# Three stages of a two-block transformer begin the next stage's dense product before they end

## What is computed

```
hn = rmsnorm(h)
proj = hn @ w_in                                   # dq dk dv dz da db sq sk sv gate_dn gate_sb
o_dn = rmsnorm(gated_delta_rule(q, k, v, g, beta)) * silu(dz)          # 8 heads of 256, in two groups
o_sb = stick_breaking_attention(rmsnorm(sq), rmsnorm(sk), sv)          # 8 heads of 128
merged = sigmoid(gate_dn) * (o_dn @ w_branch_dn) + sigmoid(gate_sb) * (o_sb @ w_branch_sb)
h = h + merged @ w_out
h = h + (silu(gate) * up) @ w_ffn_out              # gate, up = rmsnorm(h) @ w_ffn_in
```

## Time and profile before

| | |
|---|---|
| median of 3 runs | 2320.32 us (2319.63 to 2327.05) |
| span of the profiled execution | 2316.6 us |
| PE busy | 2205.7 us, 95% |
| DVE busy | 1116.4 us, 48% |
| ACT busy | 806.4 us, 35% |
| transfers | 218.65 MB, mean 94 GB/s |

### The profile page before, as it was taken

The page is one execution under the profiler, slowest core; times in us unless marked ns, Lnnn a source line. Parts: engine busy times, 40 slices in busy tenths (PEclk is TensorE's granted clock), DMA queues, the critical chain, the costliest instruction groups (busy, mean ns, idle before and its releaser), DMA issues. The chain is left out here.

```text
span 2316.6 us, 32721 instructions
## 1 busy us (share of the span) xinstructions
PE 2205.7 (95%) x13572; PEld 1700.6 (73%) x13572; DVE 1116.4 (48%) x1800; ACT 806.4 (35%) x1310; POOL 67.8 (3%) x88
## 2 busy tenths in 40 slices
PE   8999799999999999989998999998999999999999
PEld 7776457777778898976765788766566578888887
DVE  3464675666653367654334534436332244444422
ACT  3332554333332443332224222225346533223221
POOL 0000001000000000000000000000012102000000
PEclk8999899999999999999999999999999999999999
DMA  4224001222232244331224321214721232322322
GB/s 161 65 72 154 1 1 64 82 91 82 87 105 92 78 145 130 124 110 59 66 69 146 130 92 62 70 55 150 247 69 55 91 115 91 95 96 91 98 94 91
DMA packets 78595, 218.65 MB, mean 94 GB/s; under 512 B 8688, under 2 KB 13168, under 8 KB 78448
## 3 DMA queue, kind: packets, MB, share of 16 engines
q1 hardware_dynamic: 78448, 216.57, 28.2%
HBM read 185.74 MB, written 29.75 MB: 93 GB/s over the span
## 5 line engine op out<-in xcount | busy, mean ns | idle before, releaser
L296 PE MATMUL ps<-nx_hi,whi 128*128 128x264 f32 (+1 forms) x1504 | 539.1, 358 | 17.0 <-DVE nx_lo L385 9.6
L281 DVE TENSOR_TENSOR wlo<-raw,whi 128x1024 fp32r<-128x1024 f32 x282 | 346.3, 1228 | 400.4 <-ACT whi L274 400.0
L298 PE MATMUL ps<-nx_hi,wlo 128*128 128x264 f32 (+1 forms) x1504 | 512.9, 341 | 0.0
L297 PE MATMUL ps<-nx_lo,whi 128*128 128x264 f32 (+1 forms) x1504 | 512.8, 341 | 0.0
L274 ACT ACTIVATE whi<-raw 128x1024 fp32r<-128x1024 f32 x282 | 297.8, 1056 | 520.9 <-PE ps L298 416.5
L296 PEld LDWEIGHTS ps<-nx_hi,whi 128*128 128x128 f32 x1504 | 287.0, 191 | 84.6 <-issue 45.3
L298 PEld LDWEIGHTS ps<-nx_hi,wlo 128*128 128x128 f32 x1504 | 287.1, 191 | 32.6
L297 PEld LDWEIGHTS ps<-nx_lo,whi 128*128 128x128 f32 x1504 | 287.7, 191 | 30.4 <-issue 1.9
L296 PE MATMUL ps<-x_hi,whi 128*128 128x512 f32 x528 | 209.8, 397 | 14.9 <-DVE wlo L281 14.9
L298 PE MATMUL ps<-x_hi,wlo 128*128 128x512 f32 x528 | 209.8, 397 | 0.0
L297 PE MATMUL ps<-x_lo,whi 128*128 128x512 f32 x528 | 208.4, 395 | 0.0
(11 more groups left out here) (460 smaller groups left out, 2869.9 us busy)
## 6 DMA issues: line engine op xcount, KB each, us to landing
raw<-stream_dram SPq DMA_DIRECT2D x285, 512.0 KB, 3.5
qk_spill<-ring SPq DMA_DIRECT2D x16, 264.0 KB, 2.2
qk_cols<-qk_spill SPq DMA_DIRECT2D x16, 264.0 KB, 4.0
v_spill<-ring SPq DMA_DIRECT2D x16, 264.0 KB, 2.1
v_cols<-v_spill SPq DMA_DIRECT2D x16, 264.0 KB, 4.3
dz_spill<-ring SPq DMA_DIRECT2D x16, 256.0 KB, 2.1
dz<-dz_spill SPq DMA_DIRECT2D x16, 256.0 KB, 5.1
sbk_spill<-ring SPq DMA_DIRECT2D x8, 264.0 KB, 2.1
```

The costliest lines, as they stand in the source:

```text
L281: dve.tensor_tensor(K.wlo[:, n % HL], K.raw[:, n % RAW], K.whi[:, n % HL].bitcast(F32), ALU.subtract).then_inc(K.s_lo, 1)
L296: pe.matmul(out, whi, xhi, start=start, stop=False, skip_group_check=skip)
L297: pe.matmul(out, whi, xlo, start=False, stop=False, skip_group_check=skip)
L298: return pe.matmul(out, wlo, xhi, start=False, stop=stop, skip_group_check=skip)
```

## The change

A new lane, `Begun`, stands in three stages. It issues matmuls of the next stage's first two outputs with six of their eight contraction tiles (at the end of DeltaOutput 0, 2, 1, 3, 4 and 6, the first that it makes; else 0 to 5), 18 for each output, without a stop, and the next stage's product leaves these out and ends the sums: 6 matmuls for each of its first two outputs. The three places are the end of DeltaOutput (for SecondBranch), of StickBreaking (for LastBranch) and of LastBranch (for `out_ffn`). `Begun` waits for the chunk, for the bank, and for each contraction tile. At the end of DeltaOutput and StickBreaking the banks are 6 and 7, which the stage's own dense product must have left; in LastBranch they are 0 and 1, and nothing holds them. In StickBreaking the first of the two outputs has a time just before the last values, the other one behind all.

So that the operand of LastBranch is there in time, StickBreaking now makes both parts itself: ACT copies a head's bank into `o_hi`, DVE takes the difference of bank and `o_hi` into `o_lo`, two heads at a time. SplitOutputs, with its 8 copies and 8 differences, is gone, and so are the waits of LastBranch's first output. No load is moved from one stage to another.

```diff
...
 
-def out_ffn(K, x_hi, x_lo, nk, conv, gain_ffn, gain_next, out):
+def out_ffn(K, x_hi, x_lo, nk, conv, gain_ffn, gain_next, out, begun=None):
 
...
                     bank_free(d)
-                    for k in range(nk):
+                    skipped = begun.over(s) if begun is not None else ()
+                    for k in range(len(skipped), nk):
                         w = slice((w0 + k) * P, (w0 + k + 1) * P)
                         mm = three(pe, K.ps[:, d % 4, :], K.whi[:, s % HL, w], K.wlo[:, s % HL, w], x_hi[:, k], x_lo[:, k],
-                                   k == 0, k == nk - 1)
+                                   k == 0, k == nk - 1, len(skipped) > 0)
                     if d % per == per - 1:
...
 
-    def __init__(self, K, n, operand, banks, z, t0, t1, led=0):
+    def __init__(self, K, n, operand, banks, z, t0, t1, led=0, begun=None):
         super().__init__(t0, t1)
+        self.begun = begun
         self.K, self.first, self.n, self.operand, self.banks, self.led = K, K.at, n, operand, banks, led
...
                 q = self.base[c] + h
-                for k in range(KT):
+                skipped = self.begun.over(s) if self.begun is not None else ()
+                left = [k for k in range(KT) if k not in skipped]
+                for k in left:
                     yield self.at((c + (h + k / KT) / len(rng)) / self.n)
-                    if h == 0 and k == 0:
+                    if h == 0 and k == left[0]:
                         pe.wait_ge(K.s_lo, s + 1)
-                    if k == 0 and q >= len(self.banks):
+                    if k == left[0] and q >= len(self.banks):
                         pe.wait_ge(self.free, q - len(self.banks) + 1)
                     mm = three(pe, K.ps[:, self.bank(c, h), 0:e - a], K.whi[:, s % HL, k * P:(k + 1) * P],
-                               K.wlo[:, s % HL, k * P:(k + 1) * P], xh[:, k, a:e], xl[:, k, a:e], k == 0, k == KT - 1, True)
+                               K.wlo[:, s % HL, k * P:(k + 1) * P], xh[:, k, a:e], xl[:, k, a:e], k == 0, k == left[-1], True)
                 if h == len(rng) - 1:
...
 
+class Begun(Lane):
+
+
+
+    def __init__(self, K, x_hi, x_lo, a, e, tiles, ready, outs):
+        super().__init__(1e6, 1e6)
+        self.K, self.x_hi, self.x_lo, self.a, self.e = K, x_hi, x_lo, a, e
+        self.tiles, self.ready, self.outs, self.first = tiles, ready, outs, K.at
+
+    def over(self, s):
+        return self.tiles if s < self.first + len(self.outs) else ()
+
+    def pe(self, pe):
+        K = self.K
+        for q, (bank, t, free) in enumerate(self.outs):
+            s = self.first + q
+            yield t
+            pe.wait_ge(K.s_lo, s + 1)
+            if free is not None:
+                pe.wait_ge(*free)
+            for i, k in enumerate(self.tiles):
+                pe.wait_ge(self.ready, i + 1)
+                three(pe, K.ps[:, bank, 0:self.e - self.a], K.whi[:, s % HL, k * P:(k + 1) * P], K.wlo[:, s % HL, k * P:(k + 1) * P],
+                      self.x_hi[:, k, self.a:self.e], self.x_lo[:, k, self.a:self.e], i == 0, False, True)
+
+
 class Stored(Products):
...
 
+    def tile_order(self):
+        return [2 * (2 * j + p) + f for j, f, p in self.ORDER]
+
     def sp(self, sp):
...
 
-    def __init__(self, K, o_hi, o_lo, first_part, gate, dst, c, banks, z, t0, t1):
+    def __init__(self, K, o_hi, o_lo, first_part, gate, dst, c, banks, z, t0, t1, begun):
         self.src, self.dst = (first_part, gate), dst
...
         self.loaded, self.taken, self.stored = [z["branch_in_0"], z["branch_in_1"]], z["branch_taken"], [z[s] for s in STORED_SEMS]
-        super().__init__(K, 8, lambda c: (o_hi, o_lo, [(0, SEQ)]), banks, z, t0, t1)
+        super().__init__(K, 8, lambda c: (o_hi, o_lo, [(0, SEQ)]), banks, z, t0, t1, begun=begun)
 
...
 
-STICK_SEMS = ("z", "ln", "softplus", "later", "log_w", "sw", "pv", "so")
+STICK_SEMS = ("z", "ln", "softplus", "later", "log_w", "sw", "pv", "so_hi", "so")
 
...
 
-    def __init__(self, K, qT, kT, v, z, c, t0, t1):
+    def __init__(self, K, qT, kT, v, o_hi, o_lo, z, c, t0, t1):
         super().__init__(t0, t1)
-        self.K, self.qT, self.kT, self.v, self.s = K, qT, kT, v, z
+        self.K, self.qT, self.kT, self.v, self.o_hi, self.o_lo, self.s = K, qT, kT, v, o_hi, o_lo, z
         self.units = [x for h in range(0, SB_H, 2) for x in [(h + j, a) for j in range(2) for a in (3, 2, 1, 0)] + [(h, TT)]]
...
         K, s = self.K, self.s
+
+        def copy_lo(h):
+            dve.wait_ge(s["so_hi"], h + 1)
+            dve.tensor_tensor(self.o_lo[:, h], K.ps[:, 3 + h % 3, :], self.o_hi[:, h].bitcast(F32), ALU.subtract).then_inc(s["so"], 1)
         for u in range(self.NU):
...
                                      ALU.max, ALU.add).then_inc(s["softplus"], 1)
+            if u >= self.PER and u % self.PER == 2:
+                for j in range(2):
+                    copy_lo(2 * (u // self.PER - 1) + j)
+        yield self.t1
+        for j in range(2):
+            copy_lo(SB_H - 2 + j)
 
...
             act.wait_ge(s["pv"], self.PER * (h // 2 + 1))
-            act.activation(self.qT[:, h, 0:SEQ], K.ps[:, 3 + h % 3, :], ACT.Copy).then_inc(s["so"], 1)
+            act.activation(self.o_hi[:, h], K.ps[:, 3 + h % 3, :], ACT.Copy).then_inc(s["so_hi"], 1)
         act.preload_act_table_set("natural_log_exp_and_others")
...
 
-class SplitOutputs(Lane):
-
-
-    def __init__(self, K, src, hi, lo, z, t0, t1):
-        super().__init__(t0, t1)
-        self.K, self.src, self.hi, self.lo, self.made, self.done = K, src, hi, lo, z["so_hi"], z["so_lo"]
-
-    def act(self, act):
-        for i in range(8):
-            act.activation(self.hi[:, i], self.src[:, i], ACT.Copy).then_inc(self.made, 1)
-        yield from ()
-
-    def dve(self, dve):
-        for i in range(8):
-            dve.wait_ge(self.made, i + 1)
-            dve.tensor_tensor(self.lo[:, i], self.src[:, i], self.hi[:, i].bitcast(F32), ALU.subtract).then_inc(self.done, 1)
-        yield from ()
-
-
 class LastBranch(Products):
...
 
-    def __init__(self, K, o_hi, o_lo, merged, gate, c, banks, z, t0, t1):
+    def __init__(self, K, o_hi, o_lo, merged, gate, c, banks, z, t0, t1, begun):
         self.src = (merged, gate)
...
         self.s = z
-        super().__init__(K, 8, lambda c: (o_hi, o_lo, [(0, SEQ)]), banks, z, t0, t1)
-
-    def pe(self, pe):
-        for k, t in enumerate(super().pe(pe)):
-            if k < KT:
-                pe.wait_ge(self.s["so_lo"], k + 1)
-            yield t
+        super().__init__(K, 8, lambda c: (o_hi, o_lo, [(0, SEQ)]), banks, z, t0, t1, begun=begun)
 
...
             z = named_sems(K, PRODUCT_SEMS, STORED, OUT_SEMS)
-            together(K, DeltaOutput(K, S, o_hi, o_lo, D2["dz"], 8, z, c2, 0, 8),
-                     Stored(K, [(8, XQ, D2["gdn"], 0, rs, (ACT.Tanh, 0.5))], ring, (6, 7), z, 0, 8, 1))
+            output = DeltaOutput(K, S, o_hi, o_lo, D2["dz"], 8, z, c2, 0, 8)
+            dense = Stored(K, [(8, XQ, D2["gdn"], 0, rs, (ACT.Tanh, 0.5))], ring, (6, 7), z, 0, 8, 1)
+            begun = Begun(K, o_hi, o_lo, 0, SEQ, output.tile_order()[0:6], z["o_free"], [(6, 1e6, (dense.free, 7)), (7, 1e6, (dense.free, 8))])
+            together(K, output, dense, begun)
         qT = S.v.rearrange("p m j n -> p (m j n)").rearrange("p (h t) -> p h t", h=8)
...
                 z = named_sems(K, PRODUCT_SEMS, STORED, NORM_COL_SEMS, VALUE_SEMS, ("branch_in_0", "branch_in_1", "branch_taken"))
-                dense = SecondBranch(K, o_hi, o_lo, D2["br0"], D2["gdn"], D2["pre"], c3, (6, 7), z, 0, 8)
+                dense = SecondBranch(K, o_hi, o_lo, D2["br0"], D2["gdn"], D2["pre"], c3, (6, 7), z, 0, 8, begun)
                 together(K, NormCols(K, [(kT[:, i], par(K, "sbk_gain")) for i in range(8)] + [(qT[:, i], par(K, "sbq_gain")) for i in range(8)],
...
                 z = named_sems(K, PRODUCT_SEMS, STORED, STICK_SEMS)
-                together(K, StickBreaking(K, qT, kT, v_rows, z, c3, 0, 8),
-                         Stored(K, [(8, XQ, D2["gsb"], 0, rs, None)], ring, (6, 7), z, 0, 8, 1))
+                dense = Stored(K, [(8, XQ, D2["gsb"], 0, rs, None)], ring, (6, 7), z, 0, 8, 1)
+                begun = Begun(K, o_hi, o_lo, 0, SEQ, range(6), z["so"], [(6, 7.99, (dense.free, 7)), (7, 1e6, (dense.free, 8))])
+                together(K, StickBreaking(K, qT, kT, v_rows, o_hi, o_lo, z, c3, 0, 8), dense, begun)
         with ExitStack() as c2:
-            z = named_sems(K, PRODUCT_SEMS, ("so_hi", "so_lo", "gate_sig", "m_sum", "m_hi", "m_lo"), tuple(f"merge_in_{i}" for i in range(8)))
-            together(K, SplitOutputs(K, qT, o_hi, o_lo, z, 0, 8), LastBranch(K, o_hi, o_lo, D2["pre"], D2["gsb"], c2, (6, 7), z, 0, 8))
-    out_ffn(K, K.nx_hi[:, :, META:T2], K.nx_lo[:, :, META:T2], KT, False, par(K, "g_ffn2"), None, v["out"])
+            z = named_sems(K, PRODUCT_SEMS, ("gate_sig", "m_sum", "m_hi", "m_lo"), tuple(f"merge_in_{i}" for i in range(8)))
```

(4 more changed lines are left out.)

## The result

The changed kernel takes 2329.09 us (median of 16 runs, 2325.07 to 2338.81), the kernel before, run beside it, 2323.10 us (16 runs, 2319.45 to 2327.41). The ratio is 1.0028, 95% interval 1.0017 to 1.0039: 6.5 us more (the two medians alone are 6.0 apart), at the upper edge of what was called no difference. The sum had said +4.9 us, on the 2320.32 us known then.

The account below looks back on a forecast made before the run. PE, busy 95% of the span, was taken as the bound, so gains come only from its stands and half-rate stretches. A +4.5, B +6.5, C -6.1 sum to +4.9 us on median 2320.32: 2325.2 us, range 2317 to 2331.

Parts of the forecast that it names:

- A: End of DeltaOutput to SecondBranch: +4.5 us, bounds +3.5 (loads alone) and +6.6 (third output at half rate).
- B: End of StickBreaking to LastBranch: +6.5 us, bounds +4.5 (transfers 2 us quicker) and +8.1 (half rate in second begun output).
- C: End of LastBranch to out_ffn: -6.1 us, as nothing holds the 36 begun matmuls.
- 1.0 (0.45 + 3 x 0.19): At A, the us by which half rate stretches the sums and 3 matmuls before the first evacuation.
- rival 1: Half rate decides: A costs 6.6 and B 8.1 us, sum +8.6, 2328.9 us; chance 22%.
- A sigmoid sooner than 9 us: Sign of being wrong at B: LastBranch's first sigmoid sooner than 9 us after its opening; 9.3 was forecast.
- near 1854: Sign of being right: LastBranch's first tile loads issued near 1854 (1849.9 plus A's 4.5).
- The split inside StickBreaking: Six differences added on DVE inside StickBreaking fall into gaps and cost nothing; 1.2 us each pair if uncovered.
- Rival 2: Stands simply filled at all three ends: gains of 5.4 at A, 4.1 at B, 6.1 at C, -15.6, 2304.7; 9%.
- Rival 3: Loads land sooner after an opening, 3 us at A and 2 at B: +1.5 + 3.1 - 6.1 = -1.5, 2318.8; 7%.
- The -1.5 us: Sum in place of +4.9 if a 256 KB tile landed after 2.6 us, an estimate from the skill page.

Follow-up runs that it names:

- e1: The kernel before with begun outputs only at LastBranch to out_ffn, ends A and B and the outputs' split as before; ratio 0.9976 to the kernel before.
- e3: The kernel before with the outputs' split moved into StickBreaking and begun outputs only at StickBreaking to LastBranch; ratio 1.0038 to the kernel before.
- e4: The kernel before with begun outputs only at DeltaOutput to SecondBranch; split, B and C as before; ratio 1.0018 to the kernel before.
- e5: The changed kernel with the last gate output's evacuation put ahead of the last two differences on DVE; ratio 1.0022 to the kernel before.
- e6: The changed kernel with LastBranch's first two weight loads issued after the tiles of its first two and first four outputs; ratio 1.0018 to the kernel before.
- e10: The changed kernel with e5's order, LastBranch's first two outputs' tiles loaded in StickBreaking, its first two weight loads put first; ratio 0.9956 to the kernel before.
- e9: The changed kernel with the tiles of SecondBranch's first six squares loaded a stage ahead, in DeltaOutput; ratio 0.9998 to the kernel before.
- e2: The changed kernel without any begun output, so only the outputs' split moves into StickBreaking; ratio 1.0008 to the kernel before.
- e11: The changed kernel with the edits of e9 and e10 together; ratio 0.9942 to the kernel before, median 2311.59 against 2326.37.

## Why the prediction was right, and where it was off

- **Verdict and sum.** No difference over 0.3% was right by little: +6.5 us (3.9 to 9.1) where +4.9 stood and 7.0 was the line, and the local sum, +7.1, is past it. The measured median, 2329.1, lies in the range though 3.9 above the forecast, 2.8 of which the kernel before had moved too (2320.32 to 2323.10). The mechanism was right: the signs of all three terms, and what PE waits for at A and B; e1, e3 and e4 show each term alone. The sizes were helped by luck: at A and at B half rate cost more than was put down, and the loads landed sooner than was put down, which took part of it back.
- **C, -6.1**: 6.1 in the changed kernel, 6.3 alone.
- **A, +4.5, came as +5.4.** In before's time (the lag of 7.89 taken off) the stage opens at 1626.9 against 1627.0 predicted; the first square starts at 1633.2 against 1633.85; the third output at 1645.6, against 1645.2. What was mis-sized is the half rate, "1.0 (0.45 + 3 x 0.19)". The sixth square came sooner than predicted (1642.3 for 1642.85), but from its start to the third output it took 3.3 us and not 2.3, since PE, at half rate, still had the fifth square's sum and three matmuls ahead of the sixth's sum. Half rate then reaches 1.1 us into the third output, another 0.5. Together 1.0 + 0.5 - 0.6 (the sooner square) = 0.9 over the +4.5. How far half rate reaches differs from profile to profile, and A with it: a clock of 0.50 over the 13 us behind the first sum goes with +5.4 and +5.5 (the change, e4), 0.70 with +4.7 (e5), 0.85 and 0.88 with +3.7 and +3.8 (e6, e10), end A being the same in all five. Why it differs is open. The bounds of 3.5 and 6.6 hold them all.
- **B, +6.5, came as +7.7.** The step that failed is the one sentence "after a longer stand of 2.69 us and behind it the clock held 1.00, so I take full rate". The stand came as predicted (2.67 for 2.6), but behind it 8 of the 18 matmuls ran at half rate, 1.5 us, and the stage opened that much later; so it did in all five kernels that have this stand (0.62 to 0.76 over the second begun output), and where e5 took the stand away, the clock was 1.00. This half of rival 1 came true. Against it, LastBranch's first sigmoid ended 7.9 us after the opening and not 9.3, so that the stand was 5.76 and not 7.3, and the fourth output began 18.8 us after it and not 19.3. "A sigmoid sooner than 9 us" had been named as a sign of being wrong, and it came: the loads that release it took 5.6 us from the opening here and 6.0 to 6.5 in e3 and e5 to e9, against 7.0 in before. Why they are quicker was not tested. LastBranch opened at 1857.0 in before's time, where "near 1854" stood: 0.9 for A, 1.6 for the half rate.
- **The split inside StickBreaking, nothing**: e2 shows nothing there.
- **Rival 2**, the stands simply filled, -15.6: not what this change does, but its price was nearly right. With the loads a stage ahead e11 gives -14.1.
- **Rival 3**, loads that land 3 us sooner at A and 2 at B, fell: counted from the opening they came 0.6 and 1.4 sooner. Its sum was wrong besides. It takes +3.1 for B, where the bound worked out above for transfers 2 us quicker is +4.5; with this the rival is 1.5 + 4.5 - 6.1 = -0.1 us, which is no other verdict than the forecast's. The fourth tile of LastBranch was issued at 1866.20 and released the table load at 1870.45, 4.2 us later, with the other tiles in the same engines (DMA share 0.79 from the opening to there). By the Trainium skill, page "DMA: Bandwidth & Descriptors", section "Anatomy of one DMA — SWDGE (gpsimd) path", a tile of 256 KB would land in 2.6 us, an estimate from its fit for one DMA of GpSimd's queue; this trace does not agree with it for tiles in a burst from SP. The -1.5 us given beside that estimate in the prediction is the same wrong sum.

## What to carry to other kernels

Work that is pulled in front of a stage's end fills a stand only if the next stage has something else to do while its own loads come: the matmuls that were moved had been covering them, and the loads are still issued where the stage opens. At C it had (the first load issued there was not needed before the fourth output), and the stand was filled at no cost; at A and B it had not. There, move the first loads with the work, or move neither. In every queue that a moved step enters, ask what stands ahead of it: one evacuation behind two differences on DVE was worth 3.7 us here, one square behind a late weight split on ACT made a stand of 2.1.

## What the runs showed that I had not expected

**A stand of 2.7 us can go either way with the clock.** The stand of the earlier trace rows, in a stage far from the change, has the same length in all 14 profiles, 2.69 or 2.70 us. Behind it the clock held in 6 of them (before, e1, e4, e6, e9, e10) and fell in 8. After, stand and window; before's window beneath:

```profile
885.16 0.71 PE L1143 MATMUL ps<-rt,const_sb 32*128 32x264 f32 x4 [2.70 <-DVE rt L1153]
...
887.00:893.00 6.00, 6.00 (x26) 0.50 0.39 132
```

```profile
886.00:892.00 6.00, 6.00 (x43) 1.00 0.37 132
```

It costs 4.5 us where it falls (4.5 to 4.6 in eight profiles, 0.0 in the five others beside before). I had drawn from the one execution in which it held that such a stand is safe. It is also most of what the changed kernel had lost before it reached A: 1.2 us stood before it, 4.5 are its own, and 2.2 came between it and A, where nothing was changed either. And it says what a profile pair is worth: the runs of before themselves differ by more than the change. Of the 35 beside e1 to e4, 11 took 2319.0 to 2322.2 us, with a mean granted clock of 0.979 to 0.981, and 24 took 2324.3 to 2334.1 us, with 0.973 to 0.977. The middles of the two groups are some 7 us apart. That this stand makes the groups was not shown; with 4.5 us it can't be all of it.

**SP issues sixteen loads in 8.5 us.** From LastBranch's opening at 1864.89 they go out about 0.5 us apart, and the first weight load behind them at 1873.38:

```profile
1864.89 0.32 SPq L1994 DMA_DIRECT2D merge_in<-pre_spill  x1
...
1873.38 9.89 SPq L261 DMA_DIRECT2D raw<-stream_dram  x3
```

Its split starts at 1880.59. For this load the 8.5 us in which SP issued the others are more than the 7.2 us from its own issue to the split.
